# Opening of a two-layer decoder kernel: first weight tiles in two pieces, two buffers of squares, rotary angles ahead of the first tiles

## The chip, the cores and the metric

The kernel runs on one core of a Trainium2 chip. The metric is the device time of one launch in microseconds (us). Before the change it is 2274.3 us, the median of three runs (2273.61 to 2274.34).

## What is computed

A causal decoder trunk of two layers over 1024 tokens of width 1024, all in float32. Only the start of layer 0 matters here: the RMS norm of x, the rotary tables, and the first columns of the combined projection.

```python
def rms_norm(x, g):
    y = xf * lax.rsqrt(jnp.mean(xf * xf, axis=-1, keepdims=True) + RMS_EPS)
    return (y * g)

def rope_tables(positions, dim):
    inv_freq = ROPE_THETA ** (-jnp.arange(0, dim, 2) / dim)
    ang = positions[..., None] * inv_freq
    return jnp.cos(ang), jnp.sin(ang)

def pool_diffattn_layer(x, cos, sin, ...):
    z = rms_norm(x, norm_g) @ w_in
    a = pool_mixer(z[..., :POOL_WIDTH], pool_w, pool_scale)
    b = diff_attention(z[..., POOL_WIDTH:], cos, sin, q_g, k_g, lam, lam_init, subln_g)
    return jnp.concatenate([a, b], axis=-1) @ w_out

for layer in range(2):
    x = x + (pool_diffattn_layer or mlstm_layer)(x, ...)
    x = x + conv_ffn(x, ...)
```

## The kernel before, in words

**Number format.** Every large product is made of three matmuls of reduced-precision parts. A weight tile (128 x 1024, 512 KB) is loaded to `w_raw`, rounded to `w_hi`, and the rest is `w_lo = w_raw - w_hi`; x is split in the same way into `xa_hi` and `xa_lo`. A product is `w_hi*x_hi + w_lo*x_hi + w_hi*x_lo`. The profile names the moving operand first, so `pj<-xa_hi,w_lo` is the second of these.

**Layout.** x lies transposed in memory, as eight chunks `x_first[c]` of 128 channels x 1024 tokens. A weight tile holds 128 output channels: its columns `k*128` to `k*128+127` are multiplied with chunk k. Six matmuls of 512 columns (three products, two halves of the tokens) make one group (tile, chunk), and eight groups one tile. The division by the root mean square comes after the product, so the matmuls of a tile only wait for the split of x. Squares of the chunks are summed in `ssum` and reduced on TensorE.

**Who does what in the opening.** The five engines follow hand-written instruction orders, coupled by semaphores.

- SyncE (SP) issues the loads in this order: weight tile 0, the parameters (`s_par`), x chunks 0 to 2, weight tile 1, x chunks 3 to 7, then constants, inverse frequencies, lambda vectors, the other parameters, the positions (`s_pos`), and weight tiles 2, 3, and on. Tiles 3 and 4 wait until tiles 0 and 1 are split.
- ScalarE (ACT) in `act_mixer0`: rounds tile 0 (`act_first_cut`, L940), makes `xa_hi` of chunks 0 to 2 (`act_norm_high`, L392), rounds tile 1, squares chunk 0, and then alternates `high(c)` and `square(c - 2)` (L400). A square after the second waits until VectorE has added the one before, as there is one buffer, `sq_tmp`. After them come the angle and the number of whole turns (L969, L971), tile 2, the last squares, sine and cosine (L977, L979, which load another table), and the two stores of these tables by ACT's own queue (L982).
- VectorE (DVE) in `dve_mixer0`: the rest of tile 0 (`dve_first_cut`, L946), four small parameter products (L1145 to L1148), `xa_lo` of chunks 0 to 2 (`dve_norm`, L404), the rest of tile 1, and then `xa_lo` of a chunk and one addition of squares (`add_squares`, L412) by turns. The whole turns are taken off the angle (`dve_turns_off`, L1097), it is folded into one period (`dve_fold`, L1101 and L1102, twice) and limited (L1107) between the last additions.
- TensorE (PE) in `pe_mixer0`: ten matmuls of ones (L809) and eight on the rounded tile 0 (L812) whose results are not used, then the groups of tiles 0 and 1 (`pe_group`, L347). Tile 1 runs two chunks behind tile 0 (`LAG = 2`). Then the sums of squares (`pe_stat`, L364), tile 2 in units of two chunks (L325), the norm's second step (L368), and on into attention.
- GpSimd (POOL) splits the weight tiles from the third on (tile 3, L1661 and L1663), once tiles 0 to 2 are done.

```python
            for k in range(KC + LAG):
                if k < KC:
                    pe_group(pe, 0, 0, X, k, k == 0, k == KC - 1, *ready, k + 1)
                if k >= LAG:
                    pe_group(pe, 1, 1, X, k - LAG, k == LAG, k == KC + LAG - 1)
            pe.wait_ge(s_const, 16 * N_CONST)
            pe_stat(pe, 0, 0)
```

After the tables are stored, SP reads them back in another layout (`sp_tables`, L601), and DVE needs them for the first rotation (L570).

Of the kernel before, what the change touches and what calls it, by code (L numbers as in the profile page):

```python
# [7 lines left out]
F32 = mybir.dt.float32  # L8
# [12 lines left out]
SQ = S // 4  # L21
HEADS = 4
# [50 lines left out]
def program(nc, x_in, pos_in, wall, pool_w, params, lam4, consts, invf, scratch, out):  # L73
    with ExitStack() as ctx:
# [7 lines left out]
        def at(name, shape, dt, offset):  # L82
            return nc.alloc_sbuf_tensor_at(name, shape, dt, offset=offset)
# [64 lines left out]
        ang = at("angle", [P, SQ], F32, r_b + 9 * K4)  # L148
        turn = at("turns", [P, SQ], F32, r_b + 10 * K4)
        turni = at("turns_int", [P, SQ], I32, r_b + 11 * K4)  # L150
        red = at("angle_reduced", [P, SQ], F32, r_b + 12 * K4)
        redc = at("angle_size", [P, SQ], F32, r_b + 13 * K4)
        sinq = at("sin_packed", [P, SQ], F32, r_b + 13 * K4 + 1024)
        cosq = at("cos_packed", [P, SQ], F32, r_b + 13 * K4 + 2048)
# [37 lines left out]
        def sem(name):  # L192
            return ctx.enter_context(nc.semaphore(name))
# [18 lines left out]
        N_CONST = 5  # L212
        s_const = sem("s_const")
        s_par = sem("s_par")
        s_xin = [sem(f"s_xin{c}") for c in range(KC)]
# [177 lines left out]

        def act_norm_square(act, ph, c, src):
# [12 lines left out]
        def add_squares(eng, ph, c):  # L407

            eng.wait_ge(norm_sq[ph], c + 1)
            if c > 1:  # L410
                eng.wait_ge(norm_acc[ph], c - 1)
            eng.tensor_tensor(ssum[:, :], ssum[:, :], sqt[:, :], ALU.add).then_inc(norm_acc[ph], 1)  # L412
# [21 lines left out]
        tab_in = sem("tab_in")  # L434
        angle_in = sem("angle_in")
# [369 lines left out]
        def pe_mixer0(pe):  # L805
# [4 lines left out]
            pe.wait_ge(w_high, 1)  # L810
            for i in range(N_WARM[1]):
                pe.matmul(dn[:, 1, 0:HALF], whi[:, 0, 0:P], whi[:, 0, 0:HALF], start=True, stop=True)  # L812
# [135 lines left out]
        def act_mixer0(act):

            act_first_cut(act, 0)  # L950
            act.wait_ge(s_par, 16)
            act.wait_ge(set_dve, 4)
# [6 lines left out]

            for c in range(3):  # L960
# [173 lines left out]
        def dve_mixer0(dve):  # L1134
# [25 lines left out]
            add_squares(dve, 0, KC - 1)  # L1160
            dve_first_cut(dve, 2)
# [1308 lines left out]
        def _(sp):  # L2470
            sp_load(sp, 0, 0)
            sp.dma_start(par[:, 0:PC_FFN], params[:, 0:PC_FFN]).then_inc(s_par, 16)
            for c in range(3):
                sp.dma_start(xin[:, c, :], x_in[c, :, :]).then_inc(s_xin[c], 16)
            sp_load(sp, 1, 1)
            for c in range(3, KC):
                sp.dma_start(xin[:, c, :], x_in[c, :, :]).then_inc(s_xin[c], 16)
            sp.dma_start(idt[:, :], consts[0, :, 0:P]).then_inc(s_const, 16)
            sp.dma_start(cst[:, :], consts[0, :, P:(1 + N_CB) * P]).then_inc(s_const, 16)
            sp.dma_start(invc[:, :], invf).then_inc(s_const, 16)  # L2480
            sp.dma_start(lamt[:, :], lam4).then_inc(s_const, 16)
            sp.dma_start(par[:, PC_FFN:N_PC], params[:, PC_FFN:N_PC]).then_inc(s_const, 16)
            sp.dma_start(posi[:, :], pos_in).then_inc(s_pos, 16)
# [184 lines left out]
```

## Time and profile before

| what | value |
|---|---|
| median of three runs | 2274.3 us (2273.61 to 2274.34) |
| the profiled execution, its own time | 2274.28 us |
| its span | 2272.5 us |
| TensorE busy | 2261.0 us, 99% of the span |
| VectorE busy | 1190.7 us, 52% |
| GpSimd busy | 882.0 us, 39% |
| ScalarE busy | 572.2 us, 25% |
| chain that ended last | TensorE 95%, VectorE 3% |
| DMA | 132.29 MB, mean 58 GB/s |

The span runs from the first to the last instruction of one profiled execution; the 1.8 us between it and the execution's own time lie outside the instructions. "L347" is line 347 of the program. The chain that ended last is followed back from the last instruction to whatever released each step. Matmuls are pipelined, so a matmul's own duration is longer than the distance to the next one. SPq and ACTq are the DMA queues that SyncE and ScalarE issue into.

### The profile page before, as it was taken

The page shows a single profiled execution, that of the slowest core. Times are in us where ns is not written, and L with a number is a line of the kernel's source. Part 1 is how long each engine was busy: PE and PEld are TensorE (multiplying, and loading weights), DVE is VectorE, ACT ScalarE, POOL GpSimd, SP SyncE. Part 2 cuts the span into 40 slices and gives each one's busy share as a digit, 9 for nine tenths or more (in the row PEclk, how much of TensorE's full clock was granted, in tenths as well). Part 3 has the DMA queues.
Part 4 walks back from the last instruction along what each step waited for, and adds up shares of the span by engine and source line. Part 5 has one row for each costly group of instructions (what it writes and reads, how often), then busy time and mean ns, then how long its engine had stood idle before and what let it go on. Part 6 is the DMA issues. An engine that isn't in the chain of part 4 may idle for free.

```text
span 2272.5 us, 27216 instructions
## 1 busy us (share of the span) xinstructions
PE 2261.0 (99%) x10747; PEld 1870.7 (82%) x10747; DVE 1190.7 (52%) x1176; ACT 572.2 (25%) x888; POOL 882.0 (39%) x395
## 2 busy tenths in 40 slices
PE   9999999999999999999999999999999999999999
PEld 7777778888888888888888898788888888888887
DVE  7776763464554555545644144444545555554554
ACT  5555441221111111111344333422111111111110
POOL 1212226444334433344643333275344433443342
PEclk9999999999999999999999999999999999999999
DMA  5111121111111111111321111031111111111111
GB/s 195 56 47 47 33 92 57 47 47 49 54 46 46 46 54 47 46 47 53 115 79 56 35 59 65 21 135 45 51 47 46 46 55 46 46 46 52 50 47 74
DMA packets 38721, 132.29 MB, mean 58 GB/s; under 512 B 4912, under 2 KB 6768, under 8 KB 38640
## 3 DMA queue, kind: packets, MB, share of 16 engines
q1 hardware_dynamic: 35760, 122.24, 16.7%
q10 hardware_dynamic: 2880, 8.91, 1.0%
q8 instruction: 58, 0.95, 0.2%
q14 instruction: 23, 0.19, 0.0%
HBM read 118.26 MB, written 8.68 MB: 56 GB/s over the span
## 4 chain that ended last, share of the span: by engine, by line
PE 95%; DVE 3%; issue 1%; ACT 0%; DMA 0%; SPq 0%; ACTq 0%; DVEq 0%
PE pj L1367 42%; PE dn L1387 17%; PE pj L347 15%; PE pj L325 6%; PE pj L1860 3%; PE dn L1438 3%; PE dn L686 1%; PE pj L712 1%; PE pj L1438 1%; PE pj L506 1%; PE pj L696 1%; PE dn L1998 1%; PE dn L2007 1%; PE dn L1886 1%; PE pj L1886 1%
## 5 line engine op out<-in xcount | busy, mean ns | idle before, releaser
L1661 POOL TENSOR_TENSOR w_hi<-w_raw,ones 128x1024 fp32r<-128x1024 f32 x186 | 356.0, 1914 | 1329.9 <-PE pj L1367 564.0
L1663 POOL TENSOR_TENSOR w_lo<-w_raw,w_hi 128x1024 fp32r<-128x1024 f32 x186 | 468.3, 2518 | 14.6
L1491 DVE SCALAR_TENSOR_TENSOR ffn_y<-ffn_h,params,ffn_y 128x1024 f32<-128x1024 f32 x176 | 323.6, 1838 | 117.6 <-ACT ffn_y L1499 109.0
L1499 ACT ACTIVATE ffn_y<-ffn_h,params 128x1024 f32<-128x1024 f32 x88 | 109.6, 1245 | 886.6 <-DVE ffn_h L1480 886.6
L1480 DVE TENSOR_TENSOR ffn_h<-pj,rms_bc 128x1024 f32<-128x1024 f32 x88 | 107.8, 1225 | 365.5 <-PE pj L1367 351.9
L1540 DVE TENSOR_TENSOR res<-dn,res 128x1024 f32<-128x1024 f32 x144 | 176.1, 1223 | 115.4 <-PE dn L1387 115.4
L1367 PE MATMUL pj<-xb_hi,w_hi 128*128 128x512 f32 x704 | 216.9, 389 | 0.0
L1367 PE MATMUL pj<-xa_hi,w_hi 128*128 128x512 f32 x704 | 216.9, 389 | 0.0
L1367 PE MATMUL pj<-xb_hi,w_lo 128*128 128x512 f32 x704 | 216.7, 389 | 0.0
L1367 PE MATMUL pj<-xa_hi,w_lo 128*128 128x512 f32 x704 | 216.7, 389 | 0.0
L1367 PE MATMUL pj<-xa_lo,w_hi 128*128 128x512 f32 x704 | 216.7, 389 | 0.0
L1367 PE MATMUL pj<-xb_lo,w_hi 128*128 128x512 f32 x704 | 216.7, 389 | 0.0
L1387 PE MATMUL dn<-act_hi_buf,w_hi 128*128 128x512 f32 x576 | 177.3, 389 | 0.0
L1387 PE MATMUL dn<-act_lo_buf,w_hi 128*128 128x512 f32 x576 | 177.3, 389 | 0.0
L1387 PE MATMUL dn<-act_hi_buf,w_lo 128*128 128x512 f32 x576 | 177.3, 389 | 0.0
L1367 PEld LDWEIGHTS pj<-xa_hi,w_lo 128*128 128x128 f32 x704 | 132.2, 188 | 27.4
L1367 PEld LDWEIGHTS pj<-xb_hi,w_lo 128*128 128x128 f32 x704 | 132.2, 188 | 27.4
L1367 PEld LDWEIGHTS pj<-xb_lo,w_hi 128*128 128x128 f32 x704 | 132.2, 188 | 27.4
L1367 PEld LDWEIGHTS pj<-xa_lo,w_hi 128*128 128x128 f32 x704 | 132.2, 188 | 27.4
L1367 PEld LDWEIGHTS pj<-xb_hi,w_hi 128*128 128x128 f32 x704 | 132.0, 188 | 27.3
L1367 PEld LDWEIGHTS pj<-xa_hi,w_hi 128*128 128x128 f32 x704 | 132.0, 188 | 27.2
L347 PE MATMUL pj<-xb_hi,w_hi 128*128 128x512 f32 x384 | 128.3, 415 | 0.0
(321 smaller groups left out, 3550.4 us busy)
## 6 DMA issues: line engine op xcount, KB each, us to landing
w_raw<-weights SPq DMA_DIRECT2D x189, 512.0 KB, 3.5
x_first<-x_t SPq DMA_DIRECT2D x8, 512.0 KB, 9.8
res<-x_t SPq DMA_DIRECT2D x8, 512.0 KB, 6.8
scratch<-res ACTq DMA_DIRECT2D x8, 512.0 KB, 2.6
res<-scratch SPq DMA_DIRECT2D x8, 512.0 KB, 8.4
y_t<-res ACTq DMA_DIRECT2D x7, 512.0 KB, 2.6
q_turned<-q_raw SPq DMA_DIRECT2D x16, 128.0 KB, 2.3
k_turned<-k_raw SPq DMA_DIRECT2D x16, 128.0 KB, 2.3
```

The source lines that it names most:

```text
L325: ins = pe.matmul(o, w, x[:, k, t * HALF:(t + 1) * HALF], start=(k == 0 and m == 0), stop=(k == KC - 1 and m == 2))
L347: ins = pe.matmul(o[:, t * HALF:(t + 1) * HALF], w, x[:, k, t * HALF:(t + 1) * HALF], start=(first and m == 0), stop=(last and m == 2))
L1367: ins = pe.matmul(o[:, t * HALF:(t + 1) * HALF], w[:, wsl, k * P:(k + 1) * P], x[:, k, t * HALF:(t + 1) * HALF], start=(k == 0 and q == 0) ...
L1387: ins = pe.matmul(dn[:, d % 2, t * HALF:(t + 1) * HALF], w[:, wsl, at0:at0 + P], x[:, 2 * (s % 2) + e, t * HALF:(t + 1) * HALF], start=(e ...
L1438: ins = pe.matmul(o[:, t * HALF:(t + 1) * HALF], w[:, wsl, at0:at0 + P], x[:, x0, t * HALF:(t + 1) * HALF], start=(i == 0 and q == 0), sto ...
L1480: dve.tensor_tensor(h[:, SH:SH + S], pj[:, js, :], rbc[:, :], ALU.mult).then_inc(pj_free[js], 1)
L1491: dve.scalar_tensor_tensor(y[:, :], h[:, SH - lag:SH - lag + S], f.tap(j, m, q), y[:, :], ALU.mult, ALU.add).then_inc(taps[f.l], 1)
L1499: act.activation(f.y[m][:, :], f.h[m][:, SH:SH + S], ACT.Identity, bias=f.tap(j, m, 3), scale=f.tap(j, m, 2)).then_inc(center[f.l], 1)
L1540: dve.tensor_tensor(res[:, d, :], dn[:, d % 2, :], res[:, d, :], ALU.add).then_inc(dn_free[d % 2], 1)
L1661: pool.tensor_tensor(whi[:, w, :], raw[:, r, :], ones[:, 0:1].to_broadcast([P, D]), ALU.mult).then_inc(w_high, 1)
L1663: pool.tensor_tensor(wlo[:, w, :], raw[:, r, :], whi[:, w, :].bitcast(F32), ALU.subtract).then_inc(w_ready, 1)
L1860: ins = pe.matmul(value_bank(h, b), XB[mine][:, x, b * P:(b + 1) * P], theirs[:, wsl, w], start=(t == 0 and k == 0 and q == 0 and b % 2 == 0),
```

## The change

- SP now loads the first 384 columns of tile 0, x chunks 0 to 2, the first 384 columns of tile 1, the other 640 columns of tile 0, x chunk 3, the other 640 of tile 1, x chunk 4, and then chunks 5 to 7. 384 columns are what chunks 0 to 2 need (`FIRST = 3 * P`).
- The parameters, the positions and the inverse frequencies are issued by ACT, as its first three instructions, and have semaphores of their own.
- Each split of tiles 0 and 1 is in two pieces. TensorE waits for the first piece at chunk 0 and for the second at chunk 3. The eight unused matmuls read 384 columns instead of 512.
- ACT makes angle and whole turns right after the first piece of tile 0 and ahead of `high(0)`. DVE takes the turns off and folds once ahead of its first `xa_lo`, folds a second time and limits ahead of `xa_lo` of chunk 3.
- In this norm a second buffer `sq_second` takes the even squares; a square waits for the addition two back instead of one. The squares start after `high(4)`.
- The sine and cosine come after the last square, and SP issues the stores of the tables. POOL also waits for the last addition of squares, which on DVE comes before the split of tile 2 that POOL waited for already. The buffers of the angles are packed closer, to make room.

```diff
         def pe_group(pe, n, j, X, k, first, last, hi_sem=None, lo_sem=None, landed=None):

-            if first:
+            if n in (0, 1):
+                if first:
+                    pe.wait_ge(first_ready, n + 1)
+                if k * P == FIRST:
+                    pe.wait_ge(w_ready, n + 1)
+            elif first:
                 pe.wait_ge(w_ready, n + 1)
                 pe_take(pe, j)
...
         def act_norm_square(act, ph, c, src):
             if c == 0:
                 act.activation(ssum[:, :], src, ACT.Square).then_inc(norm_sq[ph], 1)
             else:
-                if c > 1:
-                    act.wait_ge(norm_acc[ph], c - 1)
-                act.activation(sqt[:, :], src, ACT.Square).then_inc(norm_sq[ph], 1)
+                ahead = 2 if ph == 0 else 1
+                if c > ahead:
+                    act.wait_ge(norm_acc[ph], c - ahead)
+                act.activation(squares_of(ph, c)[:, :], src, ACT.Square).then_inc(norm_sq[ph], 1)
...
         def act_mixer0(act):

+            act.dma_start(par[:, 0:PC_FFN], params[:, 0:PC_FFN]).then_inc(s_par, 16)
+            act.dma_start(posi[:, :], pos_in).then_inc(s_pos, 16)
+            act.dma_start(invc[:, :], invf).then_inc(s_inv, 16)
             act_first_cut(act, 0)
...
+            def angles():
+                act.wait_ge(s_pos, 16)
+                act.wait_ge(s_inv, 16)
+                act.activation(ang[:, :], posi[:, :], ACT.Copy, scale=invc[:, 0:1]).then_inc(turn_in, 1)
+                act.wait_ge(turn_in, 1)
+                act.activation(turni[:, :], ang[:, :], ACT.Copy, scale=1.0 / (2 * math.pi)).then_inc(turn_in, 1)
+
+            angles()
             act.wait_ge(s_par, 16)
             act.wait_ge(set_dve, 4)
...
             for c in range(3):
                 high(c)
             act_first_cut(act, 1)
+            act_rest_cut(act, 0)
+            high(3)
+            act_rest_cut(act, 1)
+            high(4)
             square(0)
-            for c in range(3, KC):
+            square(1)
+            for c in range(5, KC):
                 high(c)
-                square(c - 2)
...
+                square(c - 3)
+            square(KC - 3)
             square(KC - 2)
-            act_first_cut(act, 2)
+            act_rest_cut(act, 2, 0)
             square(KC - 1)
...
+            sines()
...
+            dve_turns_off(dve)
+            dve_fold(dve, ALU.is_gt, math.pi, -2 * math.pi)
             for c in range(3):
                 dve_norm(dve, 0, c, XA, xin[:, c, :])
             dve_first_cut(dve, 1)
-            for c in range(3, KC):
-                dve_norm(dve, 0, c, XA, xin[:, c, :])
-                add_squares(dve, 0, c - 2)
-            dve_turns_off(dve)
-            add_squares(dve, 0, KC - 2)
-            dve_fold(dve, ALU.is_gt, math.pi, -2 * math.pi)
+            dve_rest_cut(dve, 0)
             dve_fold(dve, ALU.is_lt, -math.pi, 2 * math.pi)
             dve_reduced(dve)
-            add_squares(dve, 0, KC - 1)
-            dve_first_cut(dve, 2)
+            dve_norm(dve, 0, 3, XA, xin[:, 3, :])
+            dve_rest_cut(dve, 1)
+            dve_norm(dve, 0, 4, XA, xin[:, 4, :])
+            add_squares(dve, 0, 1)
+            for c in range(5, KC):
+                dve_norm(dve, 0, c, XA, xin[:, c, :])
+                add_squares(dve, 0, c - 3)
+            for c in range(KC - 3, KC):
+                add_squares(dve, 0, c)
+            dve_rest_cut(dve, 2, 0)
...
         @block.sync
         def _(sp):
-            sp_load(sp, 0, 0)
-            sp.dma_start(par[:, 0:PC_FFN], params[:, 0:PC_FFN]).then_inc(s_par, 16)
+            sp_first_load(sp, 0)
             for c in range(3):
                 sp.dma_start(xin[:, c, :], x_in[c, :, :]).then_inc(s_xin[c], 16)
-            sp_load(sp, 1, 1)
-            for c in range(3, KC):
+            sp_first_load(sp, 1)
+            sp_rest_load(sp, 0)
+            sp.dma_start(xin[:, 3, :], x_in[3, :, :]).then_inc(s_xin[3], 16)
+            sp_rest_load(sp, 1)
+            sp.dma_start(xin[:, 4, :], x_in[4, :, :]).then_inc(s_xin[4], 16)
+            for c in range(5, KC):
                 sp.dma_start(xin[:, c, :], x_in[c, :, :]).then_inc(s_xin[c], 16)
```

ACT's queue of instructions from the start, before the change (names as in the profile; `w_hi<-w_raw` is a rounding of a weight tile, `xa_hi` that of x):

```order
L940 ACT_TABLE_LOAD
L940 ACTIVATE w_hi<-w_raw 128x1024
L392 ACTIVATE xa_hi<-x_first,params 128x1024 x3
L940 ACTIVATE w_hi<-w_raw 128x1024
L396 ACTIVATE ssum<-x_first 128x1024
```

and after it:

```order
L988 DMA params<-params 128x92
L989 DMA pos_int<-positions 128x256
L990 DMA inv_freq<-inv_freq 128x1
L967 ACT_TABLE_LOAD
L967 ACTIVATE w_hi<-w_raw 128x384
L1009 ACTIVATE angle<-pos_int,inv_freq 128x256
L1011 ACTIVATE turns_int<-angle 128x256
L400 ACTIVATE xa_hi<-x_first,params 128x1024 x3
L967 ACTIVATE w_hi<-w_raw 128x384
L978 ACTIVATE w_hi<-w_raw 128x640
```

Three DMA issues and the two angle instructions now stand ahead of the first `xa_hi`.

DVE's queue from the first weight split on, before the change (`w_lo` is the rest of a weight tile, `xa_lo` that of x, `ssum` the sum of squares):

```order
L946 TENSOR_TENSOR w_lo<-w_raw,w_hi 128x1024
L1145 TENSOR_SCALAR subln_scaled<-params 128x1
L1146 TENSOR_SCALAR q_gain_scaled<-params 128x1
L1147 SCALAR_TENSOR_TENSOR q_gain_turned<-params 128x1
L1148 TENSOR_TENSOR k_gain_turned<-params 128x1
L404 SCALAR_TENSOR_TENSOR xa_lo<-x_first,params,xa_hi 128x1024 x3
L946 TENSOR_TENSOR w_lo<-w_raw,w_hi 128x1024
L404 SCALAR_TENSOR_TENSOR xa_lo<-x_first,params,xa_hi 128x1024
L412 TENSOR_TENSOR ssum<-ssum,sq_tmp 128x1024
```

and after it, from the last parameter product on:

```order
L1198 TENSOR_TENSOR k_gain_turned<-params 128x1
L1147 SCALAR_TENSOR_TENSOR angle<-turns_int,angle 128x256 x3
L1151 TENSOR_SCALAR turns<-angle 128x256
L1152 TENSOR_TENSOR angle<-angle,turns 128x256
L417 SCALAR_TENSOR_TENSOR xa_lo<-x_first,params,xa_hi 128x1024 x3
L972 TENSOR_TENSOR w_lo<-w_raw,w_hi 128x384
L983 TENSOR_TENSOR w_lo<-w_raw,w_hi 128x640
L1151 TENSOR_SCALAR turns<-angle 128x256
L1152 TENSOR_TENSOR angle<-angle,turns 128x256
L1157 TENSOR_SCALAR angle_reduced<-angle 128x256
L417 SCALAR_TENSOR_TENSOR xa_lo<-x_first,params,xa_hi 128x1024
```

Five angle instructions moved ahead of the first `xa_lo`, and three more, with the second piece of tile 0, ahead of that of chunk 3.

## Rows read from the trace of the kernel before

**Rows 1.** The page: busy time of TensorE; its granted clock in 40 slices.

```profile
PE 2261.0 (99%) x10747; PEld 1870.7 (82%) x10747; DVE 1190.7 (52%) x1176; ACT 572.2 (25%) x888; POOL 882.0 (39%) x395
...
PEclk9999999999999999999999999999999999999999
```

**Rows 2.** The chain that ended last, 0 to 60 us: start us, us, what.

```profile
1.65 6.35 DMA x_first<-x_t
...
9.37 3.59 DVE xa_lo L404 x3
13.01 1.24 DVE w_lo L946
14.29 17.98 PE pj L347 x78
...
32.33 2.02 PE dn L364 x16
34.35 2.75 PE dn L325 x12
37.10 1.05 PE dn L368 x8
```

**Rows 3.** Timeline of SP's queue: start us, us, queue, line, output<-input, count.

```profile
0.74 0.39 SPq L1654 DMA_DIRECT2D w_raw<-weights  x1
1.19 0.42 SPq L2472 DMA_DIRECT2D params<-params  x1
```

**Rows 4.** Transfers issued at 1.65 and at 2.12 us: KB, us from issue to landing.

```profile
x_first<-x_t SPq DMA_DIRECT2D x1, 512.0 KB, 6.3
x_first<-x_t SPq DMA_DIRECT2D x1, 512.0 KB, 7.2
```

**Rows 5.** Timeline of DVE, 5.5 to 16.5 us.

```profile
7.34 0.16 DVE L1148 TENSOR_TENSOR k_gain_turned<-params 128x1 f32<-128x1 f32 x1
9.37 3.68 DVE L404 SCALAR_TENSOR_TENSOR xa_lo<-x_first,params,xa_hi 128x1024 fp32r<-128x1024 f32 x3 [1.87 <-ACT xa_hi L392]
```

**Rows 6.** Groups by line and form, 0 to 50 us: busy us, mean ns, idle before.

```profile
L647 DVE TENSOR_TENSOR q_raw<-pj,rms_bc 128x512 f32<-128x512 f32 x2 | 1.3, 686 | 3.3 <-ACT rms_bc L379 3.3
L1097 DVE SCALAR_TENSOR_TENSOR angle<-turns_int,angle 128x256 f32<-128x256 int32 x3 | 1.3, 423 | 0.1
L1102 DVE TENSOR_TENSOR angle<-angle,turns 128x256 f32<-128x256 f32 x2 | 0.8, 424 | 0.1
L1101 DVE TENSOR_SCALAR turns<-angle 128x256 f32<-128x256 f32 x2 | 0.6, 290 | 0.0
```

**Rows 7.** Timeline, 240 to 247 us: two issues 0.59 us apart on two queues.

```profile
241.30 0.37 ACTq L999 DMA_DIRECT2D pool_w<-pool_w_t  x1
241.89 0.33 SPq L1654 DMA_DIRECT2D w_raw<-weights  x1
```

**Rows 8.** Those two transfers, then one alone issued at 446.95 us.

```profile
pool_w<-pool_w_t ACTq DMA_DIRECT2D x1, 256.0 KB, 2.6
w_raw<-weights SPq DMA_DIRECT2D x1, 512.0 KB, 4.6
w_raw<-weights SPq DMA_DIRECT2D x1, 512.0 KB, 3.5
```

**Rows 9.** Timeline of ACT, 4 to 42 us.

```profile
25.41 0.49 ACT L969 ACTIVATE angle<-pos_int,inv_freq 128x256 f32<-128x256 int32 x1
25.93 0.42 ACT L971 ACTIVATE turns_int<-angle 128x256 int32<-128x256 f32 x1
...
34.12 1.28 ACT L374 ACT_TABLE_LOAD   x1 [0.49 <-ACT cos_packed L979]
```

**Rows 10.** Timeline of PE, 1.4 to 14.6 us.

```profile
1.48 4.58 PE L809 MATMUL dn<-ones 128*128 128x128 f32 x20 [1.48 <-DVE sel_q L1140]
5.77 2.14 PE L812 MATMUL dn<-w_hi 128*128 128x512 f32 x8
9.40 0.70 PE L347 MATMUL pj<-xa_hi,w_hi 128*128 128x512 f32 x2 [1.49 <-ACT xa_hi L392]
```

More of the change, by code:

```diff
@@ L21 @@
 SQ = S // 4
+FIRST = 3 * P
 HEADS = 4
@@ L147, in program @@
         posi = at("pos_int", [P, SQ], I32, r_b + 8 * K4)
[L148 to L154, printed above, removed]
+        ang = at("angle", [P, SQ], F32, r_b + 8 * K4 + 1024)
+        turn = at("turns", [P, SQ], F32, r_b + 8 * K4 + 2048)
+        turni = at("turns_int", [P, SQ], I32, r_b + 8 * K4 + 3072)
+        red = at("angle_reduced", [P, SQ], F32, r_b + 9 * K4)
+        redc = at("angle_size", [P, SQ], F32, r_b + 9 * K4 + 1024)
+        sinq = at("sin_packed", [P, SQ], F32, r_b + 9 * K4 + 2048)
+        cosq = at("cos_packed", [P, SQ], F32, r_b + 9 * K4 + 3072)
+        sq2 = at("sq_second", [P, S], F32, r_b + 10 * K4)
         gq8 = small("q_gain_scaled", 1)
@@ L211, in program @@
         dn_free = [sem(f"dn_free{i}") for i in range(2)]
-        N_CONST = 5
+        N_CONST = 4
         s_const = sem("s_const")
         s_par = sem("s_par")
+        s_inv = sem("s_inv")
         s_xin = [sem(f"s_xin{c}") for c in range(KC)]
@@ L392, in act_norm_high, with squares_of @@
             act.activation(X[0][:, c, :], src, ACT.Copy, scale=pc(PC_NORM + ph * KC + c)).then_inc(xt_hi[ph], 1)
+        def squares_of(ph, c):
+            return sq2 if ph == 0 and c % 2 == 0 else sqt
         def act_norm_square(act, ph, c, src):
@@ L411, in add_squares @@
                 eng.wait_ge(norm_acc[ph], c - 1)
-            eng.tensor_tensor(ssum[:, :], ssum[:, :], sqt[:, :], ALU.add).then_inc(norm_acc[ph], 1)
+            eng.tensor_tensor(ssum[:, :], ssum[:, :], squares_of(ph, c)[:, :], ALU.add).then_inc(norm_acc[ph], 1)
         qk_sq = sem("qk_sq")
@@ L434, in program @@
         tab_in = sem("tab_in")
+        first_in = [sem(f"first_in{n}") for n in range(2)]
+        first_high = sem("first_high")
+        first_ready = sem("first_ready")
         angle_in = sem("angle_in")
@@ L594, in sp_tables @@
         def sp_tables(sp):
+            for t, table in enumerate((sinq, cosq)):
+                sp.wait_ge(tabs, t + 1)
+                sp.dma_start(scratch[t, :, 0:SQ], table[:, :]).then_inc(tab_out, 16)
             sp.wait_ge(tab_out, 32)
@@ L809, in pe_mixer0 @@
                 pe.matmul(dn[:, 1, 0:P], ones[:, :], ones[:, :], start=True, stop=True)
-            pe.wait_ge(w_high, 1)
+            pe.wait_ge(first_high, 1)
             for i in range(N_WARM[1]):
-                pe.matmul(dn[:, 1, 0:HALF], whi[:, 0, 0:P], whi[:, 0, 0:HALF], start=True, stop=True)
+                pe.matmul(dn[:, 1, 0:FIRST], whi[:, 0, 0:P], whi[:, 0, 0:FIRST], start=True, stop=True)
             for k in range(KC + LAG):
@@ L935, in dve_tail, with sp_first_load, sp_rest_load, dve_first_cut @@
                               ALU.mult).then_inc(o_norm, 1)
+        def sp_first_load(sp, n):
+            sp.dma_start(raw[:, n, 0:FIRST], wall[n, :, 0:FIRST]).then_inc(first_in[n], 16)
+        def sp_rest_load(sp, n):
+            sp.dma_start(raw[:, n, FIRST:D], wall[n, :, FIRST:D]).then_inc(w_in[n], 16)
         def act_first_cut(act, n):
+            act.wait_ge(first_in[n], 16)
+            act.activation(whi[:, n, 0:FIRST], raw[:, n, 0:FIRST], ACT.Copy).then_inc(first_high, 1)
+        def dve_first_cut(dve, n):
+            dve.wait_ge(first_high, n + 1)
+            dve.tensor_tensor(wlo[:, n, 0:FIRST], raw[:, n, 0:FIRST], whi[:, n, 0:FIRST].bitcast(F32),
+                              ALU.subtract).then_inc(first_ready, 1)
+        def act_rest_cut(act, n, at0=FIRST):
             act.wait_ge(w_in[n], 16)
-            act.activation(whi[:, n, :], raw[:, n, :], ACT.Copy).then_inc(w_high, 1)
-        def dve_first_cut(dve, n):
-            dve.wait_ge(w_in[n], 16)
+            act.activation(whi[:, n, at0:D], raw[:, n, at0:D], ACT.Copy).then_inc(w_high, 1)
+        def dve_rest_cut(dve, n, at0=FIRST):
             dve.wait_ge(w_high, n + 1)
-            dve.tensor_tensor(wlo[:, n, :], raw[:, n, :], whi[:, n, :].bitcast(F32), ALU.subtract).then_inc(w_ready, 1)
+            dve.tensor_tensor(wlo[:, n, at0:D], raw[:, n, at0:D], whi[:, n, at0:D].bitcast(F32),
+                              ALU.subtract).then_inc(w_ready, 1)
         def act_mixer0(act):
+            act.dma_start(par[:, 0:PC_FFN], params[:, 0:PC_FFN]).then_inc(s_par, 16)
+            act.dma_start(posi[:, :], pos_in).then_inc(s_pos, 16)
+            act.dma_start(invc[:, :], invf).then_inc(s_inv, 16)
             act_first_cut(act, 0)
-            act.wait_ge(s_par, 16)
-            act.wait_ge(set_dve, 4)
             def high(c):
@@ L958, in square, with sines @@
                 act_norm_square(act, 0, c, xin[:, c, :])
+            def sines():
+                act.wait_ge(angle_in, 1)
+                act.activation(redc[:, :], red[:, :], ACT.Abs).then_inc(red_abs, 1)
+                act.activation(sinq[:, :], red[:, :], ACT.Sin).then_inc(tabs, 1)
+                act.wait_ge(red_abs, 1)
+                act.activation(cosq[:, :], redc[:, :], ACT.Sin, bias=halfpi[:, 0:1], scale=-1.0).then_inc(tabs, 1)
+            def angles():
[5 more added lines that the diff above has]
+            angles()
+            act.wait_ge(s_par, 16)
+            act.wait_ge(set_dve, 4)
             for c in range(3):
@@ L2506, in _ @@
             pool.wait_ge(set_dve, 4)
+            pool.wait_ge(norm_acc[0], KC - 1)
             pool.wait_ge(w_ready, 3)
```

15 lines of the change are left out of this document (removed).

## The prediction

> **What bounds the kernel now.** I read the page first. TensorE is busy 2261.0 of 2272.5 us [rows 1], so all its idle time together is 11.5 us, and no reordering can win more than that. Then I read the chain that ended last, in order of time, over the first 60 us. It shows where that idle time lies: the DMA of x chunk 0 lands at 1.65 + 6.35 = 8.0 us, three `xa_lo` on DVE run from 9.37, the split of tile 1 from 13.01, and from 14.29 the chain is TensorE without a break: 78 matmuls in 17.98 us (0.2305 each), then L364, L325 and L368 in a row [rows 2]. So what counts is when TensorE's unbroken run begins; whatever shifts it shifts the end by the same amount. The later stretches are fed by TensorE's own results and move with it.
>
> The sum is made against the profiled execution, 2274.28 us, which is the median of the runs (2274.3) to 0.02.
>
> **A ruler for the opening.** Let L be the start of DVE's first `xa_lo`, 9.37 us now [rows 2, 5]. The matmuls of tiles 0 and 1 end at 14.29 + 17.98 = 32.27, that is L + 22.90. I work out this distance after the change, and then L.
>
> **The distance from L (splits in pieces, squares in two buffers).**
> - The three `xa_lo` keep their 3.6 us [rows 2]. The split of tile 1 follows, and tile 1's first group waits for it. It took 1.23 to 1.24 us at 1024 columns [rows 2]; a DVE pass over 512 columns takes 0.686 and over 256 columns 0.424 [rows 6], so 384 columns take about 0.55. Unbroken work can begin at L + 3.6 + 0.55 + 0.05 = L + 4.2 instead of L + 4.9: 0.7 us won.
> - Ahead of `xa_lo` of chunk 3 DVE now has the 640 columns of tile 0 (between 0.686 and 1.23, say 0.8), a fold (0.29 + 0.42 [rows 6]), and the limit, an instruction of the fold's first kind (0.29). That ends `xa_lo(3)` (1.28, a third of the 3.68 us of rows 5 and a little for the overlap) at about L + 4.2 + 0.8 + 0.7 + 0.25 + 1.25 = L + 7.2. TensorE wants it after six matmuls of tile 1 and four of tile 0, at L + 4.2 + 10 x 0.2305 = L + 6.5. So it waits 0.65 us: what the smaller pieces won is nearly given back.
> - After that DVE makes a chunk in 2.4 us (`xa_lo` and an addition) against TensorE's 12 x 0.2305 = 2.8 us for two groups, and does not fall behind. The last addition of squares should end ahead of the last matmul: the angle work that stood between the last additions is gone from there. The two buffers take away waits on ACT that hid behind TensorE. Value: zero on the path, and the cover is TensorE's own 18 us.
>
> Together the end lies at L + 4.2 + 17.98 + 0.65 = L + 22.85: 0.05 us better. Bounds: 0.65 better (no wait at chunk 3), 0.5 worse (the 640 columns cost a full 1.23).
>
> **Behind the tiles.** The sines come last, so ACT loads the square root's table later in its order, but SP now issues the two stores; ACT's load stood at 34.12 before [rows 9], and with the sines begun after the last square it ends before or with TensorE's 2.02 us of L364. Then ACT has the 2.75 us of L325 for its part of the norm, as before, when L368 followed at 37.10 without a gap [rows 2]. Zero, with up to 0.5 us either way.
>
> **L itself, which decides.** Two things must be there: `xa_hi(0)`, and the angle work that DVE now does first.
> - Chunk 0. Ahead of it in the queue lay 512 + 46 KB (tile 0, parameters). Now it is 192 KB of tile 0 and, on ACT's queue, 46 + 128 KB: 192 KB less. Chunk 1, issued at 2.12, lands at 9.3 [rows 4], 1.3 us behind chunk 0, so 192 KB are 0.5 us. Chunk 0 lands at 7.5 (bounds 7.0 and 8.0).
> - The angle chain, from T, when positions and frequencies have both landed: the angle 0.5 us and the turns 0.42 on ACT [rows 9], about 1.0 with the hand-overs, then on DVE three instructions of 0.42 and a fold of 0.29 + 0.42 [rows 6]: 2.05. Together 3.1 to 3.15 us, all in front of the first `xa_lo`. DVE's gap is there: it ends its parameter products at 7.50 and begins at 9.37 [rows 5]. So L = T + 3.15, unless `xa_hi(0)` is later (7.5 + 1.25 = 8.75).
> - T is in no row. The lower bound is a small transfer without company, the 256 KB of 2.6 us [rows 8]: issued by ACT at about 1.5, frequencies would be there by 4.1. The upper bound is that they land with x chunk 1, at 7.5 + 1.3 = 8.8. Rows 7 and 8 decide for me: `w_raw` was issued by SP 0.59 us after a 256 KB transfer on ACT's queue. It took 4.6 us to land where one alone took 3.5: it stood behind the other queue's transfer. The two queues share engines, and a small transfer on its own queue has no fast lane. ACT issues parameters, positions and frequencies at about 0.75, 1.15 and 1.55 (0.37 for an issue on ACT's queue [rows 7]), SP tile 0, x chunk 0 and chunk 1 at 0.74, 1.19 and 1.65 [rows 3]. Served in order of arrival, the frequencies are behind chunk 0 and ahead of chunk 1: T = 7.6.
>
> The Trainium skill ("DMA: Bandwidth & Descriptors", Queues, rings and completion order) says that an engine serves the queues in turn and drains a whole packet of one before it switches; by that rule the frequencies come third in their queue, with chunk 1. The result of that is the second rival.
>
> **The sum.** L = 7.6 + 3.15 = 10.75, against 9.37: +1.38. Distance: -0.05. Together +1.3: 2274.28 + 1.3 = **2275.6 us**. The work that was put in DVE's gap is longer than the gap once its inputs come with chunk 0. A measurement of this kernel can tell about 0.2% (4.5 us) from no change; this is within it.
>
> **Rivals.**
> 1. *The small transfers come early* (T up to 5.6). Then the angle chain fits into DVE's gap, and L is 8.75: -0.62 - 0.05 gives 2273.6. For it: 174 KB in three transfers are little, and positions alone would need few microseconds [rows 8]. Against it: rows 7 and 8, and that chunk 0 itself needed 6.3 us from its issue [rows 4].
> 2. *Slower: the frequencies come with chunk 1* (T = 8.8). L is 11.95, +2.58 - 0.05: 2276.8. ACT holds back all `xa_hi` behind one transfer of 512 bytes. It decides against the old order from T = 6.3 on, where T + 3.15 passes 9.4. For it: taking turns by whole transfers puts it third. Against it: ACT issues a little faster than SP.
> 3. *TensorE's clock falls.* The ten unused matmuls (20 passes) of rows 10 run 0.229 us apart, the same kind in L364 0.126 (2.02 / 16) [rows 2, 10], so TensorE began at the lower level (1.2 GHz) and was at the higher (2.4 GHz) for L812, at 0.267, though the page's granted clock says full speed throughout [rows 1]. It then idled 1.49 us [rows 10] and kept its pace. Now the eight matmuls end half a microsecond earlier and L347 begins at 9.8 (forecast) or 11 us: an idle time of 2.4 to 3.5 us. If the clock falls, a stretch like the first, 4.4 us, (L809's, 1.48 to 5.8) runs at half speed, and costs 2.2: 2277.8, or 2279.0 on top of rival 2. The Trainium skill ("TensorE: Matmul & The Clock Gate", Part 1) says that a throttled clock is the default and idling brings it back; no row here shows a fall after idling.
> 4. *Nothing arrives at the end*: a wait of attention on DVE or the read-back of the tables takes up what is won or lost. Then 2274.3. Little speaks for it, since TensorE has no idle time to give there.
>
> **Chances.** Forecast 0.38; rival 1 0.35; rival 2 0.18; rival 3 0.05; rival 4 0.04. The range takes in rivals 1, 2 and 4, with half a microsecond for chunk 0's landing and the wait at chunk 3: 2273.1 to 2277.2. By the 0.2% bound: faster 0.01 (it would need 4.5 of the 9.4 us before the first real matmul), slower 0.02 (rivals 2 and 3 together), same 0.97.
>
> **What would show it.** In the profile after: the landing of the frequencies (7.6 forecast, up to 5.6 rival 1, 8.8 rival 2); an idle time of ACT ahead of the angle; the start of the first `xa_lo` at 10.75 (8.75, 11.95); a wait of TensorE of about 0.65 us at chunk 3; L364 at about 33.7 (before 32.33); the matmuls of L347 0.23 apart. I am wrong about the mechanism if DVE idles between the fold and the first `xa_lo`, and wrong about the ruler if L364's start does not move by what L moves.

## The result and the profile after

The changed kernel takes 2278.74 us (median of 17 runs), the kernel before in the same comparison 2273.89 us: ratio 1.0021, 95% interval 1.0014 to 1.0027, so 4.85 us slower. The forecast was 2275.6 us in a range of 2273.1 to 2277.2. The time lies above the range, and just past the 4.5 us that were called measurable. A few single executions took far longer (3138.89 us here, 11118.69 in e6, 3233.93 and 6960.23 of the kernel before beside e5 to e8); the ratios leave them out, and of the medians only e6's moves by more than 0.03 us (2274.39 without its long execution).

The page of the changed kernel, TensorE's busy time and granted clock (before: [rows 1]):

```profile
PE 2262.2 (99%) x10747; PEld 1871.8 (82%) x10747; DVE 1190.2 (52%) x1178; ACT 571.6 (25%) x890; POOL 882.9 (39%) x395
...
PEclk9999999999999999999999999999999999999999
```

The page hides the matter: its slices are 57 us long. The chain that ended last, over the first 130 us (start us, us, what), answers to [rows 2]:

```profile
1.67 7.39 DMA inv_freq<-inv_freq
9.15 0.52 ACT angle L1009
9.69 0.42 ACT turns_int L1011
10.21 0.44 DVE angle L1147
...
12.37 1.30 DVE xa_lo L417
13.71 23.44 PE pj L355 x92
37.15 1.78 PE dn L372 x16
38.93 2.74 PE dn L328 x12
```

Before, the chain went from x chunk 0 to the first `xa_lo` at 9.37. Now it goes through 512 bytes of inverse frequencies, through all the angle work, and reaches the first `xa_lo` at 12.37. The transfers, one by one (KB, us from issue to landing), issued at 0.75, 1.19 and 1.67 by ACT, and chunks 0, 1 and 2 issued at 1.19, 1.65 and 2.12 by SP (before: [rows 4]):

```profile
params<-params ACTq DMA_DIRECT2D x1, 46.0 KB, 2.7
pos_int<-positions ACTq DMA_DIRECT2D x1, 128.0 KB, 4.9
inv_freq<-inv_freq ACTq DMA_DIRECT2D x1, 0.5 KB, 7.4
x_first<-x_t SPq DMA_DIRECT2D x1, 512.0 KB, 4.7
x_first<-x_t SPq DMA_DIRECT2D x1, 512.0 KB, 6.1
x_first<-x_t SPq DMA_DIRECT2D x1, 512.0 KB, 7.2
```

Parameters land at 3.45, positions at 6.1, frequencies at 9.1; chunk 0 at 5.9, chunk 1 at 7.75 (8.0 and 9.3 before) and chunk 2 at 9.3. So the frequencies, issued within 0.02 us of chunk 1, land 1.3 us behind it and just ahead of chunk 2. Chunk 0 is there 2 us earlier than before, and waits 4 us for ACT, which itself waits for the frequencies (timeline of ACT):

```profile
9.15 0.51 ACT L1009 ACTIVATE angle<-pos_int,inv_freq 128x256 f32<-128x256 int32 x1 [5.18 <-DMA inv_freq<-inv_freq]
```
The timeline of TensorE, 0 to 20 us (before: [rows 10]):

```profile
5.39 1.66 PE L831 MATMUL dn<-w_hi 128*128 128x384 f32 x8
11.29 0.74 PE L355 MATMUL pj<-xa_hi,w_hi 128*128 128x512 f32 x2 [4.24 <-ACT xa_hi L400]
11.83 1.05 PE L355 MATMUL pj<-xa_hi,w_lo 128*128 128x512 f32 x2
...
17.29 1.05 PE L355 MATMUL pj<-xa_hi,w_hi 128*128 128x512 f32 x2
18.14 0.86 PE L355 MATMUL pj<-xa_hi,w_lo 128*128 128x512 f32 x2
18.84 0.63 PE L355 MATMUL pj<-xa_lo,w_hi 128*128 128x512 f32 x2
```

and busy time by stretch (stretch; its length; PE, PEld, DVE, ACT, POOL busy us with counts; granted clock; DMA share; GB/s):

```profile
7.10:11.30 4.20, 0.01 (x1) 0.04 (x1) 1.03 (x3) 2.12 (x4) 0.00 (x0) 1.00 0.97 358
11.30:13.70 2.40, 1.58 (x4) 0.77 (x4) 2.30 (x5) 2.40 (x4) 0.00 (x0) 0.61 1.04 424
13.70:18.80 5.10, 5.09 (x12) 4.02 (x13) 5.03 (x8) 5.10 (x7) 0.00 (x0) 0.52 1.04 395
18.80:37.00 18.20, 18.20 (x82) 15.03 (x81) 15.52 (x14) 13.97 (x16) 1.71 (x1) 1.00 0.28 101
```

TensorE idles 4.24 us instead of 1.49, and from the second pair of real matmuls on its clock is at the lower level (1.2 GHz): 12 matmuls in the 5.1 us from 13.7, where 22 would fit. There are two losses, then. The experiments take them apart.

### The profile page after: what moved, and what is told of

The parts are those of the page before. It is cut to its first block, busy times and chain, and to the rows that moved or that the text cites. A ratio compares the mean times of both kernels' runs of the same rounds, so it can differ in the third digit from the quotient of the medians.

```text
span 2277.0 us, 27222 instructions
## 1 busy us (share of the span) xinstructions
PE 2262.2 (99%) x10747; PEld 1871.8 (82%) x10747; DVE 1190.2 (52%) x1178; ACT 571.6 (25%) x890; POOL 882.9 (39%) x395
## 4 chain that ended last, share of the span: by engine, by line
PE 95%; DVE 3%; issue 1%; ACT 0%; DMA 0%; ACTq 0%; DVEq 0%
PE pj L1422 42%; PE dn L1442 17%; PE pj L355 15%; PE pj L328 6%; PE pj L1915 3%; PE dn L1493 3%; PE dn L705 1%; PE pj L731 1%; PE pj L1493 1%; PE pj L522 1%; PE pj L715 1%; PE dn L2053 1%; PE dn L2062 1%; PE dn L1941 1%; PE pj L1941 1%
## 5 line engine op out<-in xcount | busy, mean ns | idle before, releaser
L1718 POOL TENSOR_TENSOR w_lo<-w_raw,w_hi 128x1024 fp32r<-128x1024 f32 x186 | 468.3, 2518 | 14.6
```

The lines of the kernel that those rows point to most:

```text
L1718: pool.tensor_tensor(wlo[:, w, :], raw[:, r, :], whi[:, w, :].bitcast(F32), ALU.subtract).then_inc(w_ready, 1)
```

## The experiments

All times are medians; "before" is the kernel before in the same session. Each kernel was also profiled once. Over all profiles, the start of L364 in the first norm (L372 in the changed kernel), as the chain gives it, plus 2241.8 us gives the profiled execution's time to 0.4 us, with one exception (e2). So what happens up to there is the whole effect. The profiled execution need not be a typical one: e3's took 2273.73 us, 1.0 above its median.

| kernel | its time | before | first `xa_lo` | L364's start |
|---|---|---|---|---|
| before | | 2273.89 | 9.37 | 32.33 |
| the change | 2278.74 | 2273.89 | 12.37 | 37.15 |
| e1, 32 unused matmuls | 2276.55 | 2274.01 | 12.36 | 35.20 |
| e2, angles late | 2274.59 | 2274.01 | 6.67 | 32.83 |
| e3, frequencies by SP | 2272.76 | 2274.01 | 9.26 | 32.11 |
| e4, frequencies first | 2277.55 | 2274.01 | 11.54 | 36.00 |
| e5, angles between | 2273.10 | 2273.86 | 6.88 | 31.16 |
| e6, before without the eight | 2274.47 | 2273.86 | 9.00 | 32.88 |
| e7, before with pieces | 2273.43 | 2273.86 | 7.31 | 31.33 |
| e8, before with two buffers | 2273.71 | 2273.86 | 7.87 | 31.01 |
| e9, e3 again | 2273.07 | 2273.89 | 9.02 | 31.88 |
| e10, e5 again | 2273.47 | 2273.89 | 6.71 | 31.73 |

**e1: keep TensorE busy until its input comes.**

```diff
-        N_WARM = (10, 8)
+        N_WARM = (10, 32)
```

> The changed kernel with 32 unused matmuls on the first weight piece instead of 8, so that TensorE is busy until about 11.1 us, when the first xa_hi is ready; the angle work stays ahead of it. Theory (two losses: the angle chain starts T = 9.1 us late, and TensorE idles 4.2 us so that its clock falls): the granted clock stays full, the matmuls of tiles 0 and 1 run 0.23 us apart from the first, L364 starts at 35.2 instead of 37.0 and the kernel takes 2276.9 us (1.8 less than the change). Rival (the late angle chain makes the whole loss and the slow stretch is hidden by waits for DVE): within 0.5 us of 2278.7.

Measured: 2276.55 us (2276.25 to 2276.92), ratio to before 1.0011 (1.0002 to 1.0021), 2.2 less than the change. Its chain and its stretches:

```profile
12.36 3.68 DVE xa_lo L417 x3
19.49 15.71 PE pj L355 x68
35.20 1.78 PE dn L372 x16
```

```profile
5.40:11.30 5.90, 5.90 (x37) 5.74 (x35) 1.04 (x3) 2.13 (x4) 0.00 (x0) 1.00 0.90 321
11.30:13.70 2.40, 1.14 (x5) 0.62 (x4) 2.30 (x5) 2.40 (x4) 0.00 (x0) 1.00 1.03 419
13.70:18.80 5.10, 5.10 (x22) 4.24 (x23) 5.03 (x8) 5.10 (x7) 0.00 (x0) 1.00 1.04 395
```

The frequencies land as late as before (9.07) and the first `xa_lo` starts at 12.36, but the clock stays and 22 matmuls run where 12 did. L364 starts at 35.20, as expected, 22.84 behind the first `xa_lo`. Against the kernel before of its own session 2.5 us of loss are left, of 4.85: these are the late chain. The clock is worth the other 2.3 (1.95 by L364's start, 37.15 against 35.20).

**e2: the angle work out of the way of the first chunk.** On ACT `angles()` moves behind the last `high`; on DVE turns and folds go back among the last additions.

```diff
-            angles()
             act.wait_ge(s_par, 16)
...
+            angles()
             square(KC - 3)
...
-            dve_turns_off(dve)
-            dve_fold(dve, ALU.is_gt, math.pi, -2 * math.pi)
             for c in range(3):
                 dve_norm(dve, 0, c, XA, xin[:, c, :])
...
+            dve_turns_off(dve)
+            add_squares(dve, 0, KC - 3)
+            add_squares(dve, 0, KC - 2)
+            dve_fold(dve, ALU.is_gt, math.pi, -2 * math.pi)
+            dve_fold(dve, ALU.is_lt, -math.pi, 2 * math.pi)
+            dve_reduced(dve)
+            add_squares(dve, 0, KC - 1)
```

> The changed kernel with all angle work taken from ahead of the first xa_hi and xa_lo back among the last additions of squares; pieces, two buffers, ACT-issued parameters kept. Theory (all of the loss is the wait for the frequencies in front of chunk 0): chunk 0 lands at 5.9, the first xa_lo starts at 7.1 (12.37 in the change, 9.37 before), TensorE never idles long and keeps its clock, its matmuls of tiles 0 and 1 end at 30.2, but DVE's last addition ends only at 32.0, so that L364 starts at 32.1, 0.3 earlier than before: 2273.6 us. Rival (the pieces and the new order of the loads cost by themselves): 2275 or more.

Measured: 2274.59 us, ratio 1.0004 (0.9994 to 1.0013): 4.15 less than the change, but not faster than before. Its ten runs form two groups, six at 2273.9 to 2274.6 and four at 2275.9 to 2276.3. The profiled one is of the upper group:

```profile
32.83 2.75 PE L372 MATMUL dn<-ones,ssum 128*128 128x128 f32 x16 [1.91 <-DVE ssum L425]
```

```profile
31.00:32.80 1.80, 0.00 (x0) 0.00 (x0) 1.77 (x4) 1.20 (x2) 0.00 (x0) 1.00 0.02 5
32.80:34.00 1.20, 1.17 (x10) 1.20 (x11) 1.02 (x1) 1.19 (x3) 0.00 (x0) 0.97 0.00 0
34.00:37.00 3.00, 3.00 (x12) 2.70 (x12) 0.20 (x1) 2.53 (x4) 2.88 (x2) 0.50 0.27 89
```

The tiles end at 30.9 (30.2 was expected, although chunk 0 landed at 5.3 and the first `xa_lo` started at 6.67, earlier than expected), and TensorE waits 1.9 us for DVE's last addition. That wait was in the expectation. What was not: the clock falls behind it (0.50 granted from 34 to 37 us). The mean granted clock of each execution says the same: 0.999 in the four of the upper group, 1.000 in the six others. The fall comes at a cost of about 1.7 us in the runs where it does (the exception to the sum above: 2276.34 for the profiled execution, 1.7 more than 32.83 + 2241.8). A new wait behind the tiles takes back what an early start gives.

**e3: the frequencies by SP, behind the first piece of tile 0.** The only edit.

```diff
         def act_mixer0(act):
             act.dma_start(par[:, 0:PC_FFN], params[:, 0:PC_FFN]).then_inc(s_par, 16)
             act.dma_start(posi[:, :], pos_in).then_inc(s_pos, 16)
-            act.dma_start(invc[:, :], invf).then_inc(s_inv, 16)
...
             sp_first_load(sp, 0)
+            sp.dma_start(invc[:, :], invf).then_inc(s_inv, 16)
```

> The changed kernel with one edit: the inverse frequencies (512 bytes) are issued by SP right behind the first piece of tile 0; parameters and positions stay on ACT's queue. Theory (the queues take turns by whole transfers, and the third in ACT's queue comes behind the third in SP's): the frequencies land by 3.6, positions at 6.1 as in the change, so T = 6.1 and the first xa_lo starts at 9.3 (12.37 in the change); TensorE idles only 1.2 us and keeps its clock: 2273.6 us, 5 less than the change. Rival A (128 rows of 4 bytes are slow wherever they stand): frequencies at 7 or later, first xa_lo at 10 or later, 2275 or more. Rival B (the loss has another cause than T): near 2278.7.

Measured: 2272.76 us, ratio 0.9995 (0.9985 to 1.0004), 6.0 less than the change. Transfers issued at 1.19 (SP), 1.19 (ACT), and chunk 0, issued at 1.65:

```profile
inv_freq<-inv_freq SPq DMA_DIRECT2D x1, 0.5 KB, 2.7
pos_int<-positions ACTq DMA_DIRECT2D x1, 128.0 KB, 3.1
x_first<-x_t SPq DMA_DIRECT2D x1, 512.0 KB, 6.2
```

```profile
9.26 3.70 DVE xa_lo L417 x3
```

```profile
9.29 0.70 PE L355 MATMUL pj<-xa_hi,w_hi 128*128 128x512 f32 x2 [1.99 <-ACT xa_hi L400]
```

The same 512 bytes land at 3.9 instead of 9.1, so rival A falls. The positions land at 4.3 instead of 6.1; the large transfer that was issued beside them on SP's side now comes later. The angle chain ends at 7.5, ahead of chunk 0, and the first `xa_lo` starts at 9.26, as the expectation had it (9.3), though for another reason: chunk 0, now third, lands at 7.85. TensorE idles 1.99 us and keeps its clock. Moving this one issue of 512 bytes removes the whole loss, so rival B of this run falls. The expected 2273.6 was 0.8 too high.

**e4: the frequencies first on ACT's queue**, ahead of parameters and positions.

```diff
+            act.dma_start(invc[:, :], invf).then_inc(s_inv, 16)
             act.dma_start(par[:, 0:PC_FFN], params[:, 0:PC_FFN]).then_inc(s_par, 16)
             act.dma_start(posi[:, :], pos_in).then_inc(s_pos, 16)
-            act.dma_start(invc[:, :], invf).then_inc(s_inv, 16)
```

> The changed kernel with one edit: ACT issues the frequencies first, then parameters, then positions. Theory (turns by whole transfers): frequencies land near 3.4 with the first piece of tile 0, parameters near 5.9 with chunk 0, positions near 7.8 with chunk 1; the first xa_lo starts at 11.0. TensorE idles 2.9 us ahead of its first real matmul; if its clock stays, 2275.3 us, if it falls, 2277. Rival (small transfers are slow by their kind, not by their place): frequencies again behind chunk 1, and T as in the change, 2278.7.

Measured: 2277.55 us, ratio 1.0016 (1.0006 to 1.0026). Issued at 0.75, 1.19 and 1.67:

```profile
inv_freq<-inv_freq ACTq DMA_DIRECT2D x1, 0.5 KB, 3.2
params<-params ACTq DMA_DIRECT2D x1, 46.0 KB, 5.0
pos_int<-positions ACTq DMA_DIRECT2D x1, 128.0 KB, 6.6
```

They land at 3.95, 6.2 and 8.3; SP's first three (first piece, chunk 0, chunk 1) at 3.7, 6.0 and 7.55. Here each transfer of ACT's queue lands 0.2 to 0.75 us behind the one that SP issued at the same moment, be it 0.5 KB or 128. In the change, e1 and e2 the third lands 0.6 to 1.35 us behind SP's third (9.05 to 9.2, against 7.75 to 8.55). What decides is not the size. Whether it is the place in the queue or the moment of the issue these runs cannot say, as both engines issue at the same pace (0.75, 1.19 and 1.67 against 0.74, 1.19 and 1.65). The first `xa_lo` started at 11.54 (11.0 expected), and the time is 0.5 above the 2277 expected for a fallen clock. The clock did fall, after an idle time of 2.57 us.

**e5 and e10: a version meant to beat both.** SP issues the frequencies behind chunk 0. ACT makes angle and turns behind `xa_hi(0)`; DVE takes the turns off behind `xa_lo(0)` and folds behind `xa_lo(4)`.

```diff
-            angles()
             act.wait_ge(s_par, 16)
...
-            for c in range(3):
-                high(c)
+            high(0)
+            angles()
+            high(1)
+            high(2)
...
+            dve_norm(dve, 0, 0, XA, xin[:, 0, :])
+            dve_turns_off(dve)
+            dve_norm(dve, 0, 1, XA, xin[:, 1, :])
+            dve_norm(dve, 0, 2, XA, xin[:, 2, :])
```

> A version meant to beat both. As the changed kernel, but the frequencies are issued by SP behind x chunk 0, the angle and turns on ACT follow xa_hi(0), DVE takes the turns off between xa_lo(0) and xa_lo(1), and folds and limits after xa_lo(4). Theory (turns by whole transfers): chunk 0 lands at 5.9 as second in SP's queue, frequencies and positions by 6.3, the first xa_lo starts at 7.1, the unbroken run of tiles 0 and 1 begins at about 12.7 (14.29 before), L364 starts at 31.0 to 31.5 (32.33 before): 2272.0 to 2272.6 us. Rival (the early part wins nothing, as chunks 1 and 2 land no earlier and DVE becomes the bound behind the tiles): L364 at 32 or later, 2273.5 or more.

Measured: 2273.10 us, ratio 0.9997 (0.9987 to 1.0007). Chunk 0 landed at 5.5, frequencies at 5.95, positions at 5.7, and from its chain:

```profile
20.85 10.27 PE pj L355 x44
31.16 2.02 PE dn L372 x16
```

The mechanism came as expected (31.16 within 31.0 to 31.5), the median is 0.5 to 1.1 above what was expected. So it was run again, beside e3, with more runs.

> The kernel of e5_angles_between once more, with more runs, beside e9. Its profile had L364 at 31.16, 1.0 earlier than e3's, but its median was only 0.76 below the kernel before. Theory (the start of L364 sets the time): 1.0 us or more below the kernel before and below e9. Rival (chunk 0 as third in SP's queue lands anywhere between 6.4 and 8 us, so that one profile misleads by 1 us): e9 and e10 within 0.3 of each other.

> The kernel of e3_inv_by_sp once more, with more runs, beside e10 on the same chip. Its profile had L364 at 32.11 (before 32.33), its median was 1.25 below the kernel before. Theory (its first xa_lo waits for the angle chain or for chunk 0 as third in SP's queue, whichever is later): 0.5 to 1.3 us below the kernel before. Rival (the 1.25 was luck of one session): within 0.3.

Measured, with eleven runs each in one session: e9 2273.07 us (2272.57 to 2273.86), ratio 0.9996 (0.9987 to 1.0005); e10 2273.47 us (2273.16 to 2273.73), ratio 0.9998 (0.9989 to 1.0007); before 2273.89. In e10's profile chunks 1 and 2 landed 0.6 us later than in e5's (8.7 and 10.1 against 8.1 and 9.5) and L364 started at 31.73 instead of 31.16. So e10's theory (1.0 us or more below the kernel before, and below e9) is wrong. Its rival (within 0.3 of e9) is nearer at 0.4, though not for the reason it gave, since chunk 0 was second in this queue and landed at 5.5 and 5.3: one profile of the opening is good to about half a microsecond only. e9's 0.8 is within its theory's 0.5 to 1.3. Both versions are some 0.4 to 0.8 below the kernel before, which the intervals don't tell from no change, and e5 is not shown to be better than e3. e3 is the version to keep: 5.7 to 6.1 us faster than the change, each counted from the kernel before of its session, with one line moved.

**e6: a fall of the clock in the kernel before.** It leaves out eight matmuls whose result is not used.

```diff
-        N_WARM = (10, 8)
+        N_WARM = (10, 0)
```

> The kernel before without its eight unused matmuls on the rounded weight tile, so that TensorE idles from about 6.1 to 9.4 us, 3.3 instead of 1.5 us; everything else stands. Theory (idling ahead of the first real matmul makes the clock fall, whatever caused it): a fall of the granted clock in the profile at about 10 to 12 us, matmuls 0.43 apart for a stretch, 1 to 2.2 us more than before: 2275 to 2276.2. Rival (the clock falls in the changed kernel for another reason): 2274.0, matmuls 0.23 apart.

Measured: 2274.47 us, ratio 1.0001 (0.9992 to 1.0011). Stretches of its profile:

```profile
6.10:9.00 2.90, 0.02 (x1) 0.00 (x0) 1.18 (x5) 1.24 (x2) 0.00 (x0) 1.00 0.98 377
9.00:10.30 1.30, 1.27 (x4) 0.67 (x4) 1.30 (x2) 1.22 (x2) 0.00 (x0) 0.86 1.03 422
10.30:13.50 3.20, 3.16 (x9) 2.57 (x9) 3.20 (x3) 3.08 (x4) 0.00 (x0) 0.52 1.01 415
```

The clock falls behind 2.9 us of idling, with every other part as before. So it is the idling, and the change only caused it. The price is smaller than expected, 0.6 us by the times; from first `xa_lo` to L364 it is 0.9 (23.88 against 22.96), as chunk 0 happened to land 0.4 earlier. The stretch at the lower level is about half as long as in the change. The verdict by times alone stays open: two of the nine executions show a mean granted clock of 1.000 and are not among the fast ones (2274.79 and 2274.92). The granted clock of 0.52 decides.

**e7: the pieces alone on the kernel before.** Both tiles are loaded and split in 384 and 640 columns, all loads on SP.

```diff
-            sp_load(sp, 0, 0)
+            sp_first_load(sp, 0)
...
-            sp_load(sp, 1, 1)
+            sp_first_load(sp, 1)
+            sp_rest_load(sp, 0)
...
             dve_first_cut(dve, 1)
+            dve_rest_cut(dve, 0)
+            dve_norm(dve, 0, 3, XA, xin[:, 3, :])
+            dve_rest_cut(dve, 1)
```

> The kernel before with the two weight tiles in pieces and nothing else: loads in the order first piece of tile 0, parameters, chunks 0 to 2, the other pieces as in the change, all on SP; one buffer of squares; angles and sines where they were. The ruler of the prediction: chunk 0 about 0.5 us earlier, first xa_lo at 8.9 to 9.0, the run of the tiles ends at L + 22.85, but DVE has 1.0 us more to do (0.55 + 0.82 + 0.82 instead of 1.23) and its last addition ends at L + 23.8 = 32.8, 0.6 later than before: L364 at 32.8, 2274.5. Rival (the pieces are what makes the front faster): L364 at 31.8 and 2273.5.

Measured: 2273.43 us, ratio 0.9998 (0.9988 to 1.0008). Chunk 0, third in SP's queue behind 238 KB instead of 558, took 4.3 us to land (6.3 in [rows 4]), and the first `xa_lo` started at 7.31. L364 started at 31.33, 24.0 behind it, after TensorE had waited 0.72 us for DVE's last addition: DVE is the bound there, as the expectation had it (23.8 for its last addition). The rest of the expectation missed: it had the first `xa_lo` at 8.9 to 9.0 and 2274.5 us, and its rival's 2273.5 came out. The first `xa_lo` is 2.1 us earlier than before and L364 keeps 1.0 of it. How much of this the pieces earn is not shown: chunk 0 also landed at 6.45 without them (e8), and by the times the kernel is not told from the one before.

**e8: the second buffer alone on the kernel before.**

```diff
-                if c > 1:
-                    act.wait_ge(norm_acc[ph], c - 1)
-                act.activation(sqt[:, :], src, ACT.Square).then_inc(norm_sq[ph], 1)
+                ahead = 2 if ph == 0 else 1
+                if c > ahead:
+                    act.wait_ge(norm_acc[ph], c - ahead)
+                act.activation(squares_of(ph, c)[:, :], src, ACT.Square).then_inc(norm_sq[ph], 1)
```

> The kernel before with two buffers of squares in the first norm and nothing else (the angle buffers packed to make room). The prediction's zero: ACT's waits on DVE for the buffer (2.2 us in six waits) go away, but DVE was busy without them and the tiles take until 32.27: 2274.0, within 0.3. Rival (the buffer kept DVE waiting and it gains what DVE's last addition gains): 2273.5 or less.

Measured: 2273.71 us, ratio 1.0000 (0.9990 to 1.0009): no change, as predicted (0.29 below the expected 2274.0, 0.15 below the kernel before of its session). Its profile shows L364 at 31.01, but its loads, issued in the same order and sizes as before, happened to come early. The transfer of chunk 0, issued at 1.65:

```profile
x_first<-x_t SPq DMA_DIRECT2D x1, 512.0 KB, 4.8
```

against 6.3 in [rows 4]. The profiled execution (2273.03) is the fastest of its ten.

## Why the prediction was wrong

- **The ruler** held. The step "the end lies at L + 22.85" came out at 22.84 in e1 (35.20 - 12.36) and at 22.85 in e3 (32.11 - 9.26). In the change itself it is 24.78, and the difference is the clock. `xa_lo` of chunk 3 ended at L + 7.1 in e3 (L + 7.2 forecast), but TensorE waited there for some 0.2 us only and not 0.65: 12 matmuls lay between the split of tile 1 and that wait, where ten were counted. The end did not depend on this. The ruler says nothing where the first `xa_lo` comes early: then DVE's own work is the bound (e2, e7, with waits of 1.91 and 0.72 us).
- **Chunk 0** was put at 7.5 us with bounds of 7.0 and 8.0. It landed at 5.9. The step charged 192 KB at the 1.3 us that lay between the landings of chunks 0 and 1; the opening does not run at a steady rate. With the loads of the kernel before it landed at 6.45, 7.63 and 8.0 (e8, e6, before), so one row is no safe base.
- **T is the step that failed.** I took "served in order of arrival", put the frequencies ahead of chunk 1 and set T = 7.6. They landed at 9.1. Rows 7 and 8 let me conclude, rightly, that a small transfer has no fast lane, but they could not tell order of arrival from taking turns, and I chose. Two things were wrong. The issue was put at 1.55, ahead of chunk 1's at 1.65, and came at 1.67. And the frequencies did not land with chunk 1 (7.75) but 1.3 us behind it, with chunk 2. The order is that of rival 2, and its T of 8.8 and L of 11.95 are near the measured 9.1 and 12.37, but partly by luck: it had them land with chunk 1, whose landing it put 1.05 us too late. With the true landing of chunk 1 it would have given T = 7.75 and L = 10.9. Why they came later still is open; in e1 and e2 they landed at 9.05 and 9.2, with chunk 1 at 8.05 and 8.55. The angle chain from T took 3.3 us (9.06 to 12.37), 3.15 forecast. The Trainium skill's rule ("DMA: Bandwidth & Descriptors", Queues, rings and completion order) has an engine take turns between queues, a packet at a time. e3, e4 and the change do not contradict it, but they do not separate it from the order of issue; I had it at hand, and gave the case built on it 0.18.
- **The clock was priced as if it were independent.** Rival 3 had its own 0.05, and rivals 2 and 3 together (2279.0, within 0.3 of the result) 0.02. But the idle time follows from T: with T = 9.1 and eight unused matmuls TensorE idles 4.2 us, and the fall of the clock came with it in all sixteen executions of the comparison (mean granted clock 0.998 or 0.999; 1.000 in all ten of e1). No row before showed a fall, so rows alone could not price it; after these runs its chance under rival 2 is near one, and the range should have reached 2279. The price of 2.2 us was right (2.3 by e1's times, 1.95 by L364).
- **Whatever hides at nothing**, the sines last and the stores by SP, was right: L364's start accounts for the whole difference (37.15 - 32.33 = 4.8).

The sum by measured terms: first `xa_lo` 3.0 us later (12.37 - 9.37), the distance to L364 0.1 shorter (22.84 against 22.96), the clock 1.95 by L364's start and 2.3 by the times: 4.85 to 5.2, and 4.85 were measured.

## What to carry to other kernels

Before an engine is made to wait for a small load, look at what large transfers are issued ahead of it or beside it, in any queue: its own size says nothing (512 bytes landed at 9.1 us when issued third, at 3.9 when issued second). Fill a gap of an in-order engine with work whose inputs have landed, or put it behind the first critical instruction; otherwise the filler's inputs become the critical path, here on two engines at once. And where an idle time of TensorE grows, price the delay and the clock as one case, and read the granted clock in stretches of a few microseconds, not on the page.

## What the runs showed of the hardware that I had not expected

- Transfers of 46 and 128 KB in the second place of ACT's queue landed at 4.3 to 6.2 us, and which it was went with the second transfer of SP's queue: with 512 KB there 5.5 to 6.2 (the change, e1, e2, e4, e5, e10), with 0.5 KB there 4.3 and 4.5 (e3, e9).
- TensorE's clock fell after idle times of 1.9 us (e2, in four of ten runs by their times), 2.6 (e4), 2.9 (e6) and 4.2 (the change), and stayed after 1.5 (before) and 2.0 (e3). e2 does both, so the idle time alone does not decide. In e6 and the change the lower level showed only after the following matmuls had begun (0.86 granted in e6's first 1.3 us of work, then 0.52); in e4 it was there from the first (0.50).
- The first large loads do not land at a fixed time: the same three transfers in the same order brought chunk 0 at 6.45, 7.63 and 8.0 us in three profiles.
